# Subtracting the low halves of some weight chunks on Pool instead of DVE

## The chip, the core and the metric

The kernel runs on one core of one Trainium2 chip. The metric is the device time of one execution in microseconds (us); lower is better. TensorE is called PE here, VectorE DVE, ScalarE ACT, GpSimd Pool and SyncE SP, as in the profile.

## What is computed

256 tokens of width 1024 pass through two transformer blocks, all in float32. The first block has adaptive modulation (shift, scale, gate from a vector `c`), a mixer with three kinds of heads, and a convolved, gated feed-forward layer. The second block has grouped-query attention, a squared-ReLU MLP, bidirectional gated linear attention (GLA) and another such MLP. Cut to what matters:

```python
mod = (silu(c) @ w_ada + b_ada)                 # 6 x 1024: shift1, scale1, gate1, shift2, scale2, gate2
h = rmsnorm(x, g_mix) * (1 + scale1) + shift1
proj = h @ w_in                                 # 1024 x 2816, then three kinds of heads
x = x + (1 + gate1) * (concat(y_a, y_b, y_c) @ w_out)
...                                             # w_up 1024 x 5632, conv, silu * value, w_down
qkv = rmsnorm(h, norm_mix[0]) @ attn_w_qkv      # 1024 x 1536, attention, @ attn_w_o
...                                             # MLP: square(relu(h @ mlp_w_in)) @ mlp_w_out, 1024 x 4096
proj = rmsnorm(h, norm_mix[1]) @ gla_w_in       # 1024 x 3104, gated linear attention, @ gla_w_o
...                                             # second MLP, last rmsnorm
```

## The kernel before

**Split weights.** Every large product is made from two parts of each operand: `w_hi` is the weight rounded to PE's float32r format, `w_lo` the rest, `raw - w_hi`. The same is done with the activations. A product is three matmuls, `hi*hi + hi*lo + lo*hi` (helper `three`, lines 1444 to 1446). So a weight chunk cannot be used before its low half is there.

**Chunks.** Weights come as chunks of 1 MB, 128 partitions x 2048 float32. `STREAM` lists them in the order of their loads: 24 chunks of `w_ada`, which only DVE reads (`ada_step`, lines 942 and 945), and 139 chunks for PE (`SPLITS`): 11 of the input projection (`("in", n)`), 4 of the output projection (`out`), 33 of the first feed-forward layer (`gate`, `val`, `down`), 6 of `qkv`, 4 of `wo`, 13 of the GLA input (`gla`; the first is half as wide), 4 of `gla_out`, 64 of the two MLPs. In the input stage a chunk of `in` and one of `ada` alternate.

**The path of a chunk.** SP's queue loads it into one of 4 `raw` slots (line 455). Before it issues the load, it waits until the chunk that lay in that slot is done with: for a PE chunk until its `w_lo` is made, for an `ada` chunk until DVE has added it. SP works strictly in order, so one late slot holds all later loads. ACT copies `raw` to `w_hi` (line 483) into one of 3 split slots, which PE must have left (`chunk_used`). DVE subtracts, `w_lo = raw - w_hi` (line 823). PE then makes 48 matmuls of 128x128 by 256 with it.

**Order on the engines.** `schedule()` is one list of steps, written out by hand; every engine walks it and issues its own part of each step. At a chunk's step, ACT first makes `w_hi` of the chunk two further on (`ahead`, then `weights_upto`), and only then does its share of that step, such as the copies out of PSUM. DVE makes `w_lo` of the chunk one further on (`ahead`, then `weights_lo_upto`). So on DVE a low half stands in the queue behind all the work of the steps before it, though its `w_hi` may have been ready for long; and all that comes after it waits for it. Inside the input stage the work of the heads is woven in (`extra`): rotations (`rope`, lines 1003 to 1014), window attention (`win_a`, 1076 to 1084; `win_b`, 1112), stick-breaking (`stick_a`, 1057 and 1060). In the GLA stage it is the chain `gate(h)` that passes between ACT and DVE (lines 751 to 764 and 1318 to 1336).

**Pool.** Pool makes two memsets at the start (lines 467 and 468) and nothing else.

Of the kernel before, what the change touches and what calls it, by code (L numbers as in the profile page):

```python
# [7 lines left out]
ALU = mybir.AluOpType  # L8
ACT = mybir.ActivationFunctionType
AX = mybir.AxisListType  # L10
F32 = mybir.dt.float32
# [14 lines left out]
RAW_SLOTS = 4  # L26
SPLIT_SLOTS = 3
# [105 lines left out]
LOAD_OF = {key: n for n, key in enumerate(STREAM)}  # L133
SPLITS = [key for key in STREAM if key[0] != "ada"]
# [3 lines left out]
def schedule():  # L138
# [44 lines left out]
    for layer in range(2):  # L183
# [20 lines left out]
        for n in range(MLP_STEPS + 1):  # L204
# [14 lines left out]
LAST_USE = {0: ("in", 10), 1: ("out", 3), 2: ("val", FF_STEPS - 1), 3: ("qkv", 5), 4: ("wo", 3),  # L219
            5: ("mlp_in", 0, MLP_STEPS - 1), 6: ("gla", 12), 7: ("gla_out", 3), 8: ("mlp_in", 1, MLP_STEPS - 1)}  # L220
FIRST_USE = {("in", 0), ("out", 0), ("gate", 0), ("qkv", 0), ("wo", 0), ("mlp_in", 0, 0), ("gla_out", 0), ("mlp_in", 1, 0)}
USES = {"in": 0, "out": 1, "gate": 2, "val": 2, "qkv": 3, "wo": 4, "gla": 6, "gla_out": 7}


def build(nc, a, out, known):
# [3 lines left out]
    with ctx:  # L229
        def sb(name, shape, dt=F32):  # L230
            return ctx.enter_context(nc.sbuf_tensor(name, shape, dt))

        def sem(name):
            if name not in sems:
                sems[name] = ctx.enter_context(nc.semaphore(name))
            return sems[name]

        def mark(name, *event, by=1):

            counts[name] = counts.get(name, 0) + by  # L240
            assert (name, *event) not in marks, (name, event)
            marks[(name, *event)] = (name, counts[name])
            return sem(name), by

        def same(event, as_event):

            assert event not in marks, event
            marks[event] = marks[as_event]

        def at(*event):  # L250

            name, value = (event[0], 1) if known is None else known[0][event]
            return sem(name), value

        raw = sb("raw", [P, RAW_SLOTS, CHUNK])
        w_hi = sb("w_hi", [P, SPLIT_SLOTS, CHUNK], F32R)
        w_lo = sb("w_lo", [P, SPLIT_SLOTS, CHUNK], F32R)
# [100 lines left out]
        def wview(buf, slot, kt):  # L358
            return buf[:, slot, :].rearrange("p (k c) -> p k c", k=kt)

        def halved(buf, slot, key):

            return wview(buf, slot, KT)[:, :, 0:P] if key == ("gla", 0) else buf[:, slot, :]

        def landed(n):
            return at(f"raw_landed{n % RAW_SLOTS}", n)
# [98 lines left out]
        @block.gpsimd  # L465
        def _(pool):
            pool.memset(bqz, 0.0).then_inc(*mark("zeroed", 0))
            pool.memset(cqz, 0.0).then_inc(*mark("zeroed", 1))


        @block.scalar
# [340 lines left out]
        def _(dve):  # L812
            done = {"lo": 0}

            def weights_lo_upto(n):

                while done["lo"] <= min(n, len(SPLITS) - 1):
                    m = done["lo"]
                    key = SPLITS[m]
                    r = LOAD_OF[key]  # L820
                    dve.wait_ge(*landed(r))
                    dve.wait_ge(*at("w_hi", m))
                    dve.tensor_tensor(halved(w_lo, m % SPLIT_SLOTS, key), halved(raw, r % RAW_SLOTS, key),  # L823
                                      halved(w_hi, m % SPLIT_SLOTS, key).bitcast(F32), ALU.subtract)\
                        .then_inc(*mark("w_lo", m))
                    done["lo"] += 1

            def ahead(key, n=1):
                weights_lo_upto(SPLIT_OF[key] + n)
# [147 lines left out]
            def scaled(i):  # L977
                if i == 0:
                    weights_lo_upto(0)
                dve.wait_ge(*at("rstd", i))  # L980
                dve.wait_ge(*at("gains", 2 * i))
                for k in range(KT + 1):
                    if k < KT:
                        dve.scalar_tensor_tensor(out=y_t[:, k, :], in0=x_t[:, k, :], scalar=gain[:, i, k:k + 1],
                                                 in1=rstd[:, :], op0=ALU.mult, op1=ALU.mult)\
                            .then_inc(*mark("normed", i, k))
                    if k > 0:
                        m = 24 * i + k - 1
                        dve.wait_ge(*at("high", SET_OF_NORM[i], k - 1))
                        dve.scalar_tensor_tensor(out=h_lo[:, k - 1, :], in0=y_t[:, k - 1, :], scalar=mod[:, m:m + 1],  # L990
                                                 in1=h_hi[:, k - 1, :].bitcast(F32), op0=ALU.add, op1=ALU.subtract)\
                            .then_inc(*mark("low", SET_OF_NORM[i], k - 1))
# [432 lines left out]
        def _(pe):  # L1425
# [43 lines left out]
            def project_chunk(idx, key, tile=feature_tile, n=2):  # L1469
                if key in FIRST_USE and tile is feature_tile and n == 2:  # L1470

                    slot = weights(key)
                    dst = [take(pe, *key, m)[:, 0:S] for m in range(n)]
                    for k in range(KT):
                        operand(idx, k)
                        for m in range(n):
                            w = [wview(b, slot, KT)[:, k, m * P:m * P + P] for b in (w_hi, w_lo)]
                            ins = three(dst[m], w, (h_hi[:, k, :], h_lo[:, k, :]), k == 0, k == KT - 1)
                            if k == KT - 1:
                                ins.then_inc(*mark("job", *key, m))  # L1480
                else:
                    for m in range(n):
                        tile(idx, key, m)
                used(key, ("job", *key, n - 1))
# [122 lines left out]
            def project(kind, n):  # L1607
                project_chunk(USES[kind], (kind, n))

# [203 lines left out]
```

## Time and profile before

| what | value |
|---|---|
| three runs | 1049.38, 1051.57, 1053.0 us; median 1051.57 |
| the profiled execution | 1053.97 us, of which the span of the trace is 1052.1 |
| busy share | PE 90%, DVE 68%, ACT 48%, Pool 0% |
| mean granted clock of PE | 0.955 |

The span is the time from the first to the last instruction in the trace of one execution. Busy shares are means over stages with different limits. "Idle before" is time in which an engine did nothing, with the engine and instruction that ended it.

### The profile page before, as it was taken

The numbers are of one execution on the slowest core, as the hardware profiler recorded it, in microseconds if no ns is written. First come the engines' busy times: TensorE is split into PE (matmuls) and PEld (weight loads), VectorE is DVE, ScalarE is ACT, GpSimd is POOL, SyncE is SP. The second block draws the span as 40 slices with busy tenths as digits, with TensorE's granted clock in tenths as the row PEclk, the third lists the DMA queues.
The fourth block names the chain that finished last, engine by engine and source line by source line (L and its number), as shares of the span: only waits on it lengthen the run. The fifth ranks groups of instructions, "written<-read, shape, count | busy, mean of one in ns | idle before, by whom it ended". The sixth has DMA issues, their size and how long they took to land.

```text
span 1052.1 us, 17801 instructions
## 1 busy us (share of the span) xinstructions
PE 948.4 (90%) x7373; PEld 914.2 (87%) x7373; DVE 719.2 (68%) x1083; ACT 503.9 (48%) x713; POOL 2.9 (0%) x6
## 2 busy tenths in 40 slices
PE   4499798779999999979999999997988899999997
PEld 3498688779999998965789999997988789999997
DVE  4878586786676769886576566565885867565564
ACT  3325853444554557346554343335656554334332
POOL 1000000000000000000000000000000000000000
PEclk9689898889999999889999999998999899999999
DMA  9867446644555554330246645645442346546531
GB/s 344 309 205 258 145 160 211 229 164 158 201 171 193 193 192 134 121 90 1 81 154 209 213 169 176 214 153 160 125 144 92 98 143 211 189 164 206 192 121 41
DMA packets 122284, 177.14 MB, mean 168 GB/s; under 512 B 3088, under 2 KB 103996, under 8 KB 122076
## 3 DMA queue, kind: packets, MB, share of 16 engines
q1 hardware_dynamic: 121260, 173.97, 49.1%
q10 hardware_dynamic: 944, 2.03, 0.7%
q8 instruction: 59, 0.97, 0.4%
q14 instruction: 21, 0.17, 0.1%
HBM read 174.68 MB, written 1.05 MB: 167 GB/s over the span
## 4 chain that ended last, share of the span: by engine, by line
PE 66%; DVE 19%; ACT 5%; DMA 4%; issue 4%; SPq 1%; DVEq 0%; ACTq 0%
PE psum L1444 20%; PE psum L1445 20%; PE psum L1446 20%; DVE w_lo L823 5%; DVE ada L945 3%; DMA raw<-in_w_ada_dram 2%; PE psum L1712 1%; DMA rows<-in_g_sgu_dram 1%; PE psum L1692 1%; DVE work L862 1%; PE psum L1519 1%; ACT h_hi L494 1%; DMA raw<-in_w_out_dram 1%; DMA raw<-in_w_in_dram 1%; ACT w_hi L483 1%
## 5 line engine op out<-in xcount | busy, mean ns | idle before, releaser
L1444 PE MATMUL psum<-h_hi,w_hi 128*128 128x256 f32 x1384 | 402.2, 291 | 48.2 <-DVE w_lo L823 24.0
L1445 PE MATMUL psum<-h_lo,w_hi 128*128 128x256 f32 x1384 | 397.1, 287 | 0.0
L1446 PE MATMUL psum<-h_hi,w_lo 128*128 128x256 f32 x1384 | 396.6, 287 | 0.0
L483 ACT ACTIVATE w_hi<-raw 128x2048 fp32r<-128x2048 f32 (+1 forms) x139 | 264.4, 1903 | 173.7 <-PE psum L1446 106.7
L1444 PEld LDWEIGHTS psum<-h_hi,w_hi 128*128 128x128 f32 x1384 | 271.3, 196 | 54.1 <-issue 27.4
L823 DVE TENSOR_TENSOR w_lo<-raw,w_hi 128x2048 fp32r<-128x2048 f32 (+1 forms) x139 | 313.1, 2277 | 0.6 <-ACT w_hi L483 0.2
L1446 PEld LDWEIGHTS psum<-h_hi,w_lo 128*128 128x128 f32 x1384 | 270.8, 196 | 0.0
L1445 PEld LDWEIGHTS psum<-h_lo,w_hi 128*128 128x128 f32 x1384 | 270.7, 196 | 0.1
L1444 PE MATMUL psum<-a_hi,w_hi 128*128 128x256 f32 x688 | 192.9, 280 | 0.3 <-DVE w_lo L823 0.2
L1445 PE MATMUL psum<-a_lo,w_hi 128*128 128x256 f32 x688 | 192.3, 280 | 0.0
L1446 PE MATMUL psum<-a_hi,w_lo 128*128 128x256 f32 x688 | 192.2, 279 | 0.0
L1444 PEld LDWEIGHTS psum<-a_hi,w_hi 128*128 128x128 f32 x688 | 129.3, 188 | 0.7 <-DVE w_lo L823 0.7
L1446 PEld LDWEIGHTS psum<-a_hi,w_lo 128*128 128x128 f32 x688 | 129.3, 188 | 0.0
L1445 PEld LDWEIGHTS psum<-a_lo,w_hi 128*128 128x128 f32 x688 | 128.9, 187 | 0.0
L1183 DVE SCALAR_TENSOR_TENSOR arena<-psum,rstd 128x256 f32<-128x256 f32 x64 | 26.8, 424 | 131.2 <-PE psum L1446 130.9
L729 ACT ACTIVATE a_hi<-arena 128x256 fp32r<-128x256 f32 x64 | 26.4, 419 | 114.3 <-DVE arena L1183 114.3
L945 DVE SCALAR_TENSOR_TENSOR ada<-raw,c_act,ada 128x1024 f32<-128x1024 f32 x42 | 53.9, 1283 | 7.6 <-DMA raw<-in_w_ada_dram 6.5
L1152 DVE SCALAR_TENSOR_TENSOR arena<-psum,cols,arena 128x255 f32<-128x255 f32 x44 | 21.2, 481 | 47.2 <-ACT arena L629 33.2
L1444 PE MATMUL psum<-w_hi,h_hi 128*128 128x256 f32 x144 | 43.1, 299 | 5.8 <-DVE w_lo L823 4.1
L1445 PE MATMUL psum<-w_lo,h_hi 128*128 128x256 f32 x144 | 42.1, 292 | 0.0
L1446 PE MATMUL psum<-w_hi,h_lo 128*128 128x256 f32 x144 | 41.9, 291 | 0.0
L1444 PEld LDWEIGHTS psum<-w_hi,h_hi 128*128 128x128 f32 x144 | 29.3, 203 | 7.1 <-DVE w_lo L823 4.7
(262 smaller groups left out, 896.1 us busy)
## 6 DMA issues: line engine op xcount, KB each, us to landing
raw<-in_mlp_w_in_dram SPq DMA_DIRECT2D x32, 1024.0 KB, 5.5
raw<-in_mlp_w_out_dram SPq DMA_DIRECT2D x32, 1024.0 KB, 6.7
raw<-in_w_ada_dram SPq DMA_DIRECT2D x24, 1024.0 KB, 6.7
raw<-in_w_up_dram SPq DMA_DIRECT2D x22, 1024.0 KB, 5.2
raw<-in_gla_w_in_dram SPq DMA_DIRECT2D x12, 1024.0 KB, 5.5
raw<-in_w_down_dram SPq DMA_DIRECT2D x11, 1024.0 KB, 5.5
raw<-in_w_in_dram SPq DMA_DIRECT2D x10, 1024.0 KB, 7.6
raw<-in_attn_w_qkv_dram SPq DMA_DIRECT2D x6, 1024.0 KB, 5.2
```

Source lines behind the costliest of these rows:

```text
L483: act.activation(halved(w_hi, m % SPLIT_SLOTS, SPLITS[m]), halved(raw, r % RAW_SLOTS, SPLITS[m]), ACT.Copy).then_inc(*mark("w_hi", m))
L494: act.activation(h_hi[:, k, :], src, func, **kw).then_inc(*mark("high", idx, k))
L729: act.activation(a_hi[:, 2 * (i % 2) + f, :], ff_g[:, f, :], ACT.Square)\
L823: dve.tensor_tensor(halved(w_lo, m % SPLIT_SLOTS, key), halved(raw, r % RAW_SLOTS, key), halved(w_hi, m % SPLIT_SLOTS, key).bitcast(F32), ...
L862: dve.tensor_tensor(work[:, 0:n, :], work[:, 0:n, :], work[:, n:2 * n, :], ALU.add)\
L945: ins = dve.scalar_tensor_tensor(out=ada[:, p % 2, :], in0=src, scalar=c_act[:, k:k + 1], in1=ada[:, p % 2, :], op0=ALU.mult, op1=ALU.add)
L1152: dve.scalar_tensor_tensor(out=buf[:, f, 1:S], in0=c[:, 0:S - 1], scalar=col("conv_w1", t), in1=buf[:, f, 1:S], op0=ALU.mult, op1=ALU.add)\
L1183: dve.scalar_tensor_tensor(out=ff_g[:, f, :], in0=bank("mlp_in", layer, i, f)[:, 0:S], scalar=0.0, in1=rstd[:, :], op0=ALU.max, op1=ALU.mult)\
L1444: pe.matmul(dst, lhs[0], rhs[0], start=start, stop=False, skip_group_check=True)
L1445: pe.matmul(dst, lhs[0], rhs[1], start=False, stop=False, skip_group_check=True)
L1446: return pe.matmul(dst, lhs[1], rhs[0], start=False, stop=stop, skip_group_check=True)
L1519: ins = pe.matmul(dst[:, k:k + 1], ada[:, p % 2, k * P:(k + 1) * P], cst("ones")[:, 0:1], start=True, stop=True)
```

## The change

The low halves of the chunks of four kinds, `in`, `out`, `qkv` and `gla` (34 chunks of 139), are subtracted on Pool; DVE skips them. The other 105 stay on DVE. Pool walks the 34 chunks in the order of the stream, and waits for each one's load and its `w_hi`. PE's and SP's waits for the low half of these chunks now look at Pool's semaphore. All sizes, slots, steps and the number of instructions stay as they are.

```diff
+POOL_LOW = ("in", "out", "qkv", "gla")
...
 @block.gpsimd
 def _(pool):
     pool.memset(bqz, 0.0).then_inc(*mark("zeroed", 0))
     pool.memset(cqz, 0.0).then_inc(*mark("zeroed", 1))
+    for n, key in enumerate(SPLITS):
+        if key[0] in POOL_LOW:
+            r = LOAD_OF[key]
+            pool.wait_ge(*landed(r))
+            pool.wait_ge(*at("w_hi", n))
+            pool.tensor_tensor(halved(w_lo, n % SPLIT_SLOTS, key), halved(raw, r % RAW_SLOTS, key),
+                               halved(w_hi, n % SPLIT_SLOTS, key).bitcast(F32), ALU.subtract)\
+                .then_inc(*mark("w_lo_by_pool", n))
+            same(("w_lo", n), ("w_lo_by_pool", n))
...
 def weights_lo_upto(n):
     while done["lo"] <= min(n, len(SPLITS) - 1):
         m = done["lo"]
         key = SPLITS[m]
+        done["lo"] += 1
+        if key[0] in POOL_LOW:
+            continue
         r = LOAD_OF[key]
         dve.wait_ge(*landed(r))
         dve.wait_ge(*at("w_hi", m))
         dve.tensor_tensor(...).then_inc(*mark("w_lo", m))
-        done["lo"] += 1
```

## Rows read from the trace of the kernel before

**Rows 1.** The page's first part: busy time, share of the span, instructions.

```profile
PE 948.4 (90%) x7373; PEld 914.2 (87%) x7373; DVE 719.2 (68%) x1083; ACT 503.9 (48%) x713; POOL 2.9 (0%) x6
```

**Rows 2.** Stages: length, then busy time of PE, weight load, DVE, ACT, Pool.

```profile
54.00:105.00 51.00, 48.32 (x350) 46.97 (x351) 41.98 (x64) 20.84 (x35) 0.00 (x0) 0.90 0.73 237
105.00:150.00 45.00, 36.85 (x258) 34.38 (x257) 28.54 (x55) 33.33 (x56) 0.00 (x0) 0.89 0.54 177
150.00:200.00 50.00, 44.10 (x318) 40.71 (x316) 37.11 (x51) 18.36 (x32) 0.00 (x0) 0.90 0.61 211
404.00:462.00 58.00, 47.90 (x355) 46.19 (x355) 51.35 (x93) 26.86 (x50) 0.00 (x0) 0.92 0.39 123
715.00:840.00 125.00, 107.36 (x785) 102.76 (x784) 92.19 (x159) 71.39 (x107) 0.00 (x0) 0.93 0.38 121
```

**Rows 3.** Waits in 50:200, 404:462 and 715:840: total us, times, longest.

```profile
PE psum L1444 <- DVE w_lo L823: 8.1, 4, 3.8
...
PE psum L1444 <- DVE w_lo L823: 2.9, 2, 2.0
...
PE psum L1444 <- DVE w_lo L823: 8.1, 2, 4.1
```

**Rows 4.** PE's timeline: start, length, instruction, idle before it.

```profile
54.14 0.58 PE L1444 MATMUL psum<-h_hi,w_hi 128*128 128x256 f32 x1 [3.78 <-DVE w_lo L823]
...
90.24 0.36 PE L1444 MATMUL psum<-h_hi,w_hi 128*128 128x256 f32 x1 [2.38 <-ACT arena L573]
```

**Rows 5.** Line 1444 in windows of one chunk each (third half a chunk); PEclk follows PEld.

```profile
54.10:62.65 8.55, 5.96 (x16) 4.38 (x16) 0.64 0.76 246
63.30:69.17 5.87, 4.67 (x16) 3.00 (x16) 1.00 0.57 177
90.20:94.70 4.50, 3.08 (x8) 2.26 (x8) 0.62 1.00 354
178.60:185.90 7.30, 5.27 (x16) 3.82 (x16) 0.77 0.83 276
188.60:196.10 7.50, 5.28 (x16) 3.75 (x16) 0.77 0.81 288
422.90:431.40 8.50, 5.90 (x16) 4.38 (x16) 0.65 0.57 181
...
727.00:735.30 8.30, 5.87 (x16) 4.25 (x16) 0.66 0.79 253
780.20:787.40 7.20, 5.24 (x16) 3.77 (x16) 0.76 0.55 165
```

**Rows 6.** SP's queue, whole span, and ACT in 50:200: waits, total us, times, longest.

```profile
SPq L455 <- DVE w_lo L823: 814.5, 124, 58.9
...
ACT w_hi L483 <- DMA raw<-in_w_in_dram: 28.7, 6, 10.3
```

**Rows 7.** DVE's groups by line and form: busy us, mean ns, idle before.

```profile
L823 DVE TENSOR_TENSOR w_lo<-raw,w_hi 128x2048 fp32r<-128x2048 f32 x138 | 312.0, 2285 | 0.6 <-ACT w_hi L483 0.2 <-issue 0.2
```

**Rows 8.** Pool's timeline at the start of the span.

```profile
0.73 1.38 POOL L467 MEMSET arena<- 128x1536 f32 x1 [0.29 <-POOLq L1806]
2.04 1.38 POOL L468 MEMSET arena<- 128x1536 f32 x1
```

**Rows 9.** DVE's timeline, two places.

```profile
38.81 2.29 DVE L823 TENSOR_TENSOR w_lo<-raw,w_hi 128x2048 fp32r<-128x2048 f32 x1
41.02 0.88 DVE L984 SCALAR_TENSOR_TENSOR y_t<-x_t,gain,rstd 128x256 f32<-128x256 f32 x2
...
152.30 2.28 DVE L823 TENSOR_TENSOR w_lo<-raw,w_hi 128x2048 fp32r<-128x2048 f32 x1
```

**Rows 10.** ACT's timeline, two places in the input stage.

```profile
120.39 0.40 ACT L604 ACTIVATE arena<-arena,small 128x128 f32<-128x128 f32 x1 [2.05 <-DVE small L1084]
...
135.30 0.40 ACT L604 ACTIVATE arena<-arena,small 128x128 f32<-128x128 f32 x1 [4.78 <-DVE small L1084]
```

**Rows 11.** DVE's groups in 54:105: the low halves and the additions of `ada`.

```profile
L823 DVE TENSOR_TENSOR w_lo<-raw,w_hi 128x2048 fp32r<-128x2048 f32 x7 | 15.9, 2287 | 0.5 <-ACT w_hi L483 0.2 <-issue 0.2
L945 DVE SCALAR_TENSOR_TENSOR ada<-raw,c_act,ada 128x1024 f32<-128x1024 f32 x10 | 12.8, 1283 | 0.2
```

## The prediction

> **What bounds the kernel now.** I read the page first: PE is busy for 90% of the span, DVE for 68%, Pool for nothing [rows 1]. So over the whole span PE is the limit, and a change on another engine can only win back PE's idle time and the time it runs at the lower clock. Then I cut the span into stages. The reader should see that the stages which the change touches are not PE's best: DVE is busy for 42 of 51 us in 54:105, 37 of 50 in 150:200, 51 of 58 in the qkv stage and 92 of 125 in the GLA stage [rows 2]. Third came the list of waits, by stage: PE stood for a low half for 8.1 us in 50:200, 2.9 us in the qkv stage and 8.1 us in the GLA stage, 19.1 us in all [rows 3]. Last the timelines, for what stood in the queue. The wait at 54.14 is typical [rows 4]: DVE was in the steps before, and the low half came out of its queue late. After such an idle time PE runs at 1.2 GHz for part of the chunk: a chunk that takes 5.87 us at full clock took 8.55, 7.30, 7.50, 8.50, 8.30 and 7.20 us after these waits [rows 5].
>
> **What is taken away.** 33 subtractions of 2.285 us and a half one of about 1.2 leave DVE, 76.6 us [rows 7]. Most of it is hidden behind PE. Where it is not:
>
> 1. Start. The first low half stands in front of `y_t`, from 38.81 to 41.02, and PE waits for what follows [rows 9]: 2.2 us.
> 2. Input stage, second chunk: the wait of 3.78 and 2.7 of lower clock (8.55 less 5.87) [rows 4, 5]: 6.5 us.
> 3. The half chunk at 90.24: 2.38 idle, and 4.50 in place of 2.94 [rows 4, 5]: 4.0 us. The releaser is an ACT copy that stood behind a `w_hi` waiting for its load; loads wait for slots, which DVE frees [rows 6].
> 4. 105 to 160, where ACT's chain and then DVE's sets the order. ACT waits for `win_a` for 2.05 and 4.78 us, with a low half of 2.3 in DVE's queue ahead each time [rows 10]; one more stands at 152.30 in a stretch where DVE has no gaps [rows 9]. I take 2.05 + 2.3 + 2.2 = 6.5 us.
> 5. Output projection: of the 8.1 us of waits, 3.78 is that of item 2 and about 0.2 is small; 4.1 are left, with lower clock of 1.4 and 1.6 [rows 3, 5]: 7.1 us.
> 6. qkv: 2.9, with lower clock of 2.6 (8.50 less 5.87) [rows 3, 5]: 5.5 us.
> 7. GLA: 8.1, with 2.4 and 1.3 of lower clock [rows 3, 5]: 11.8 us.
>
> The sum is 43.6 us, if Pool's subtractions were in time everywhere and disturbed nobody.
>
> **What is added.** Pool gets 34 subtractions. The trace has none. The nearest rows are its memsets of 1536 columns, one every 1.31 us [rows 8], 0.85 ns a column for one stream, so 1.75 us for 2048. A subtraction moves three streams: if all three overlap it takes 1.75, if none does 5.2. DVE takes 2.285 for the same tile [rows 7]. I take 4.4, between two streams one after another (3.5) and three (5.2); both ends stay in the range. The Trainium skill (GPSIMD Engine Reference, 3.1) gives 4497 ns on GpSimd for such an add of 2048 float32, against 2293 on DVE; that would make the sum 34 times 0.1 us of Pool's time longer, and the trace's 2.285 agrees with its DVE half. The longer instruction alone costs little: most low halves are ready for their subtraction 5 us and more before DVE comes to it, and a PE chunk takes 5.87, so Pool keeps pace. The exception is the third chunk of the input stage, whose `w_hi` comes at about 54: its low half comes at about 58.2, PE wants it at 57: minus 1.2. No DMA is added. Behind Pool's waiting instruction only Pool's later subtractions stand; nobody else uses that queue. SP waits for Pool now where it waited for DVE, at 34 of 139 places [rows 6].
>
> **What the two engines do to each other.** This is the unknown, and it decides. No row shows Pool reading SBUF while DVE works. Below, the cost is nothing. Above, a Pool subtraction and any DVE instruction with two operands in SBUF take turns, whole instructions at a time. I see no row that puts it nearer to the lower end, and since a subtraction on either engine needs two read streams at once, I forecast the upper one. What it would then cost, stage by stage:
>
> - Start. Two Pool subtractions (in0, in1) fit into 34.9 to 43.9, and `y_t` starts at 43.9 and not at 41.02: plus 2.9 in place of minus 2.2. But the second chunk is then ready, so item 2 holds. Net minus 3.6.
> - 54:105. DVE's `ada` additions are 12.8 us, their first halves 1.5 and the two-operand parts of `rope` about 6; seven Pool subtractions are 30.8, together 51 in a stretch of 51 [rows 2, 11], where DVE's whole load had been 42. Every pause in a chain of waits now lengthens it: `ada` frees its slots some 5 us later, and SP, in order, loads behind it. I get the sixth chunk 6 us later and the stage's end 4 us later than before: plus 7.6. Item 3 is gone.
> - 105 to 160. Item 4's minus 6.5 stands against five Pool subtractions of 4.4. If the chain meets each at a random point and one in three not at all, that is 7.5 us: plus 1.
> - Output projection: minus 7.1, about 2 lost by later `ada`: minus 5.
> - qkv: minus 5.5; one instruction of the sum tree may be caught behind a Pool subtraction: plus 3. Net minus 2.5.
> - GLA: minus 11.8. In each of four `gate` chains DVE meets a subtraction, for about 1 to 2.5 us: plus 7.3. Net minus 4.5.
>
> Sum: -3.6 + 7.6 + 1 - 5 - 2.5 - 4.5 = -7.0. From the span of 1052.1 that is 1045.1, from the profiled execution's own 1053.97 it is 1047, and from the median of the runs, 1051.57, 1044.6. I forecast 1045.
>
> The Trainium skill has a rule against this change (SBUF — State Buffer, "Who interferes with whom"): a DVE instruction with two SBUF inputs contends with a GpSimd instruction that reads SBUF, and the second to issue is blocked until the first is done. No run here shows it yet. By that rule the sum is -7.0, without it -42.4.
>
> **The rivals.**
>
> *Side by side.* Pool and DVE don't hinder each other. Then 43.6 less the 1.2 comes off, but part of it turns into other waits: ACT already waits 28.7 us for loads of `in` [rows 6], and PE cannot pull those forward. I take off 8: 35 us, 1016. For it: Pool's queue is empty, all 34 low halves come early. Against: nothing in the trace.
>
> *Turns, and at the wrong moments (slower).* The mechanism is the same as in the forecast, the place is 105 to 160. There ACT's and DVE's chain has no slack, and `w_hi` of the next chunk comes from that chain, so Pool's start may fall again and again just ahead of DVE's critical instruction. If all five subtractions delay it whole, they cost 22 and not 7.5: plus 14.5, so 1059.5. It decides from three full hits on. For it: the schedule is fixed, so hits aren't random. Against: many DVE instructions there read PSUM and have only one operand in SBUF.
>
> *Nothing moves* is no case of its own: 76.6 us leave DVE for certain. That it nets to nothing lies between forecast and slower rival.
>
> **How the numbers follow.** Forecast (turns, partly hidden) 0.45, its own range 1036 to 1056; side by side 0.30, 1010 to 1030; slower rival 0.25, 1053 to 1068. What a measurement can tell from no change is 0.3%, 3 us. Faster by over 0.3% (below 1048.4): all of side by side and 0.6 of the forecast, 0.57. Slower (above 1054.7): 0.9 of the slower rival and 0.1 of the forecast, 0.28. Same: 0.15. The range of 8 in 10 leaves a third of the side-by-side case's lower half and the slower rival's top out: 1014 to 1063.
>
> **What would show it.** Pool's 34 instructions near 4.4 us (end of one to start of the next, where they queue). DVE's line 945 at 1.28 as before says side by side; a mean well above, or line 1003 with members of 4 us, says turns. The waits of PE for a low half in 50:200, qkv and GLA should be almost gone; new waits should be for `h_lo`, for `arena` and, on SP, for `ada`. The second chunk of the input stage should follow the first with no gap. The prediction is wrong if Pool's instruction is far from 4.4 us, if DVE is not slowed at all, or if its delays fall into 105 to 160.

## The result, and the profile after

The changed kernel takes 1074.36 us (median of 4 runs, 1072.7 to 1078.89); the kernel before, run beside it, takes 1052.28 (4 runs, 1049.38 to 1053.84). The ratio is 1.022, with a 95% interval of 1.018 to 1.026: slower by 2.2%. I had forecast 1045, a gain, and a range up to 1063: the time went the other way and lies above the range. The profiled execution after took 1075.56 us, with a span of 1073.7.

The first part of the page after, beside [rows 1]:

```profile
PE 952.3 (89%) x7373; PEld 913.5 (85%) x7373; DVE 739.2 (69%) x1049; ACT 503.7 (47%) x713; POOL 161.9 (15%) x40
```

DVE has 34 instructions fewer, which took 76.6 us. Its busy time was to fall from 719.2 to 642.6. It is 739.2, so what stayed on DVE takes 96.6 us longer than before. The same stages as in [rows 2], after (length, then busy time of PE, weight load, DVE, ACT and Pool, then the granted clock):

```profile
54.00:105.00 51.00, 42.53 (x319) 40.07 (x318) 46.46 (x53) 20.47 (x36) 28.38 (x6) 0.90 0.59 199
105.00:150.00 45.00, 35.26 (x237) 32.51 (x236) 27.97 (x36) 28.50 (x46) 14.05 (x3) 0.85 0.47 152
150.00:200.00 50.00, 39.87 (x302) 36.46 (x300) 40.02 (x58) 19.96 (x34) 18.06 (x4) 0.90 0.50 179
404.00:462.00 58.00, 51.31 (x395) 50.03 (x394) 49.78 (x64) 27.88 (x49) 29.29 (x6) 0.94 0.41 139
715.00:840.00 125.00, 111.75 (x847) 106.57 (x846) 84.85 (x131) 66.03 (x93) 59.91 (x13) 0.96 0.42 135
```

The stages lie up to 22 us later now, so the last two windows hold more of PE's dense work from the stage before, and the third is shifted by 12 to 18 us too. The first two compare: PE does less in each of them than before.

PE's waits after, in 50:200, in 404:462 and in 715:840 (total us, times, longest). The waits for a low half of [rows 3] have shrunk from 8.1 to 3.5 in the first stretch and are gone in the second; new ones stand in their place. In 715:840 Pool's low halves still cost 5.2 us, where DVE's had cost 8.1:

```profile
PE psum L1575 <- DVE work L1072: 6.4, 2, 5.5
PE psum L1575 <- DVE arena L1072: 4.9, 3, 2.8
PE psum L1600 <- ACT arena L608: 3.9, 1, 3.9
PE psum L1456 <- POOL w_lo L475: 3.5, 2, 2.1
...
PE psum L1456 <- DVE h_lo L866: 3.3, 1, 3.3
PE psum L1666 <- DVE work L874: 3.3, 1, 3.3
...
PE psum L1456 <- POOL w_lo L475: 5.2, 3, 3.7
```

Which instructions got longer? DVE's groups and Pool's by line and form, after (busy us, mean ns):

```profile
L957 DVE SCALAR_TENSOR_TENSOR ada<-raw,c_act,ada 128x1024 f32<-128x1024 f32 x42 | 78.4, 1867 | 3.5 <-DMA raw<-in_w_ada_dram 2.3
L1228 DVE TENSOR_TENSOR arena<-arena 64x256 f32<-64x256 f32 x16 | 19.3, 1208 | 0.5
L1335 DVE TENSOR_TENSOR work<-work 128x512 f32<-128x512 f32 x4 | 11.4, 2840 | 3.7 <-ACT work L768 3.7
L1096 DVE TENSOR_SCALAR small<-small 128x2 f32<-128x2 f32 x6 | 7.4, 1241 | 0.2
L1195 DVE SCALAR_TENSOR_TENSOR arena<-psum,rstd 128x256 f32<-128x256 f32 x64 | 26.8, 423 | 131.3 <-PE psum L1458 131.0
...
L475 POOL TENSOR_TENSOR w_lo<-raw,w_hi 128x2048 fp32r<-128x2048 f32 (+1 forms) x34 | 159.0, 4689 | 668.4 <-ACT w_hi L493 668.4
```

Before, the additions of `ada` had a mean of 1283 ns [rows 11], the rotations of L1228 one of 420, L1335 one of 692, and L1096, which handles two columns, one of 169. All of them have their operands in SBUF. Set side by side with the trace before, 26 DVE instructions stand for over 1 us, up to 4.4, and make up 92.6 of the 96.6 us. Instructions that read PSUM, such as L1195, and ACT's keep their times.

How one such meeting looks: Pool's timeline after, from 105 to 182, and DVE's in the same stretch.

```profile
109.34 4.62 POOL L475 TENSOR_TENSOR w_lo<-raw,w_hi 128x2048 fp32r<-128x2048 f32 x1 [5.32 <-ACT w_hi L493]
120.00 4.73 POOL L475 TENSOR_TENSOR w_lo<-raw,w_hi 128x2048 fp32r<-128x2048 f32 x1 [6.04 <-ACT w_hi L493]
136.89 4.70 POOL L475 TENSOR_TENSOR w_lo<-raw,w_hi 128x2048 fp32r<-128x2048 f32 x1 [12.16 <-ACT w_hi L493]
153.01 4.54 POOL L475 TENSOR_TENSOR w_lo<-raw,w_hi 128x2048 fp32r<-128x2048 f32 x1 [11.41 <-ACT w_hi L493]
159.00 4.63 POOL L475 TENSOR_TENSOR w_lo<-raw,w_hi 128x2048 fp32r<-128x2048 f32 x1 [1.45 <-ACT w_hi L493]
```

```profile
119.02 6.79 DVE L957 SCALAR_TENSOR_TENSOR ada<-raw,c_act,ada 128x1024 f32<-128x1024 f32 x2
...
135.92 6.76 DVE L957 SCALAR_TENSOR_TENSOR ada<-raw,c_act,ada 128x1024 f32<-128x1024 f32 x2
...
153.54 4.04 DVE L1112 TENSOR_TENSOR small<-small 128x12 f32<-128x12 f32 x1 [3.30 <-ACT small L619]
...
158.23 7.11 DVE L1124 TENSOR_SCALAR arena<-arena,small 128x128 f32<-128x128 f32 x12
```

A pair of `ada` additions takes 2.60 us where nobody disturbs it. The two pairs here take 6.79 and 6.76: in each, the second addition stands until Pool's subtraction, issued during the first, is done. L1112 multiplies 12 columns in 0.17 us before; here it takes 4.04, from 153.54 to 157.58, and Pool ends at 157.55. The twelve instructions of L1124 took 2.84 and take 7.11. So four of the five subtractions in this stretch hit, nearly at full length: 4.2 + 4.2 + 3.9 + 4.3 = 16.6 us.

The starts of PE's chunks say where the 21.6 us of span were lost:

| chunk | before | after | later by |
|---|---|---|---|
| first of `in` | 42.70 | 45.41 | 2.7 |
| second of `in`, its end | 62.8 | 59.07 | -3.7 |
| eighth of `in` | 104.66 | 108.40 | 3.7 |
| first of `out` | 162.39 | 180.16 | 17.8 |
| first of the feed-forward layer | 204.11 | 216.23 | 12.1 |
| first of `qkv` | 405.66 | 420.42 | 14.8 |
| first of `wo` | 510.91 | 531.29 | 20.4 |
| first of `gla` | 719.78 | 740.41 | 20.6 |
| first of `gla_out` | 833.26 | 855.72 | 22.5 |

### The profile page after: what moved, and what is told of

It reads as the page before. It is cut to its first block, busy times and chain, and to the rows that moved or that the text cites. A ratio compares the mean times of both kernels' runs of the same rounds, so it can differ in the third digit from the quotient of the medians.

```text
span 1073.7 us, 17803 instructions
## 1 busy us (share of the span) xinstructions
PE 952.3 (89%) x7373; PEld 913.5 (85%) x7373; DVE 739.2 (69%) x1049; ACT 503.7 (47%) x713; POOL 161.9 (15%) x40
## 4 chain that ended last, share of the span: by engine, by line
PE 65%; DVE 20%; ACT 6%; DMA 4%; issue 3%; POOL 1%; SPq 0%; DVEq 0%; ACTq 0%; POOLq 0%
PE psum L1456 20%; PE psum L1458 19%; PE psum L1457 19%; DVE ada L957 4%; DVE arena L1228 2%; DVE work L874 2%; ACT w_hi L493 2%; PE psum L1724 1%; DVE w_lo L836 1%; POOL w_lo L475 1%; DMA raw<-in_w_out_dram 1%; DMA rows<-in_g_sgu_dram 1%; PE psum L1704 1%; PE psum L1531 1%; DVE h_lo L866 1%
## 5 line engine op out<-in xcount | busy, mean ns | idle before, releaser
L1456 PE MATMUL psum<-h_hi,w_hi 128*128 128x256 f32 x1384 | 397.2, 287 | 41.9 <-DVE h_lo L1002 11.3
L1457 PE MATMUL psum<-h_lo,w_hi 128*128 128x256 f32 x1384 | 393.0, 284 | 0.0
L1456 PEld LDWEIGHTS psum<-h_hi,w_hi 128*128 128x128 f32 x1384 | 266.9, 193 | 47.9 <-issue 25.3
L1457 PEld LDWEIGHTS psum<-h_lo,w_hi 128*128 128x128 f32 x1384 | 266.7, 193 | 0.2
L1458 PEld LDWEIGHTS psum<-h_hi,w_lo 128*128 128x128 f32 x1384 | 266.4, 192 | 0.0
L475 POOL TENSOR_TENSOR w_lo<-raw,w_hi 128x2048 fp32r<-128x2048 f32 (+1 forms) x34 | 159.0, 4689 | 668.4 <-ACT w_hi L493 668.4
L836 DVE TENSOR_TENSOR w_lo<-raw,w_hi 128x2048 fp32r<-128x2048 f32 x105 | 236.7, 2283 | 0.0
L1195 DVE SCALAR_TENSOR_TENSOR arena<-psum,rstd 128x256 f32<-128x256 f32 x64 | 26.8, 423 | 131.3 <-PE psum L1458 131.0
L957 DVE SCALAR_TENSOR_TENSOR ada<-raw,c_act,ada 128x1024 f32<-128x1024 f32 x42 | 78.4, 1867 | 3.5 <-DMA raw<-in_w_ada_dram 2.3
```

The source lines that it names most:

```text
L475: pool.tensor_tensor(halved(w_lo, n % SPLIT_SLOTS, key), halved(raw, r % RAW_SLOTS, key), halved(w_hi, n % SPLIT_SLOTS, key).bitcast(F32), ...
L957: ins = dve.scalar_tensor_tensor(out=ada[:, p % 2, :], in0=src, scalar=c_act[:, k:k + 1], in1=ada[:, p % 2, :], op0=ALU.mult, op1=ALU.add)
L1195: dve.scalar_tensor_tensor(out=ff_g[:, f, :], in0=bank("mlp_in", layer, i, f)[:, 0:S], scalar=0.0, in1=rstd[:, :], op0=ALU.max, op1=ALU.mult)\
L1456: pe.matmul(dst, lhs[0], rhs[0], start=start, stop=False, skip_group_check=True)
L1457: pe.matmul(dst, lhs[0], rhs[1], start=False, stop=False, skip_group_check=True)
L1458: return pe.matmul(dst, lhs[1], rhs[0], start=False, stop=stop, skip_group_check=True)
```

## The experiments

My theory after the result: turns of whole instructions, as forecast, and their price is set by where on the chain each meeting falls. Rivals: Pool's 4.6 us are simply too long for the chunks; the engines share a write path or a queue and not the reads; the cost is spread evenly over the 34.

**Pool writes only.** The low halves are filled with zeros on Pool, for as long as the subtraction takes.

```diff
-pool.tensor_tensor(w_lo, raw, w_hi, ALU.subtract)
+pool.memset(w_lo, 0.0); pool.memset(w_lo, 0.0); pool.memset(first half of w_lo, 0.0)   # one after another
```

> Pool does not subtract here. For each of its 34 chunks it fills the low half with zeros, two and a half times over, so it is busy for about as long as before (2048 + 2048 + 1024 columns at 0.85 ns, 4.4 us and two short waits) but reads nothing from SBUF. The zeros leave the high-low product of these chunks out of the result; all instructions, waits and slots of the other engines stay. Theory (turns: a Pool instruction that reads SBUF and a DVE instruction with two SBUF operands exclude each other): DVE's additions of ada go back from a mean of 1.87 to 1.28 us, nothing on DVE is stretched, and the time falls to the side-by-side case, 1005 to 1030 us. Rival A (the loss is that Pool's low half comes later than DVE's would, 4.6 against 2.3 us): the time stays at 1065 to 1080, since Pool's part takes as long. Rival B (Pool's work loads SBUF whatever it does): DVE stays stretched, and the time near 1074.

This kernel leaves the product with the low halves of these chunks out.

Measured: 1017.67 us (1015.83 to 1020.82), ratio 0.9679 (0.9656 to 0.9702). DVE's and Pool's groups:

```profile
L962 DVE SCALAR_TENSOR_TENSOR ada<-raw,c_act,ada 128x1024 f32<-128x1024 f32 x42 | 53.8, 1282 | 2.6 <-DMA raw<-in_w_ada_dram 1.4
L1233 DVE TENSOR_TENSOR arena<-arena 64x256 f32<-64x256 f32 x16 | 6.7, 420 | 0.5
L1101 DVE TENSOR_SCALAR small<-small 128x2 f32<-128x2 f32 x6 | 5.3, 882 | 0.2
...
L479 POOL MEMSET w_lo<- 128x2048 f32 x33 | 60.3, 1827 | 1.9
L476 POOL MEMSET w_lo<- 128x2048 f32 x33 | 60.2, 1824 | 343.7 <-ACT w_hi L498 343.7
L482 POOL MEMSET w_lo<- 128x1024 f32 x34 | 32.6, 957 | 2.0
```

Pool is busy for 4.6 us per chunk, with the same waits in front, and the kernel gains 3.2%. So neither Pool's length nor its place in the chain costs the time: its reading of SBUF does. `ada` and the rotations are back at 1282 and 420 ns. L1101 is not: 882 against 169, though Pool reads nothing here. That is a second kind of meeting, with an instruction that has a single tensor operand; more of it at the end.

**One kind of chunk at a time.** In each, only the kinds named stay on Pool:

```diff
-POOL_LOW = ("in", "out", "qkv", "gla")
+POOL_LOW = ("in", "out")        # second kernel: ("qkv",), third: ("gla",)
```

> Only the chunks of in and out on Pool. Theory (each stage loses by itself, as the starts of PE's chunks in the two traces say: the first feed-forward chunk starts 12.1 us later in the changed kernel, and nothing there depends on qkv or GLA): before plus 12, so 1064. Rival (the loss of 22 us comes from something that Pool does as a whole, such as the granted clock or its code): plus 22 or nothing.

> Only the six qkv chunks on Pool. Theory: the delay grows by 8.3 us between the end of the feed-forward layer and the first wo chunk, so before plus 8, 1060. It splits into the sum tree that is caught behind a Pool subtraction (3.3 us of idle PE before the sum) and the rotations of q and k (line 1228, mean 1.21 in place of 0.42). Rival (those are hidden, and the shift in the trace of the changed kernel was given on from the input stage): 1047, since PE's waits of 2.9 us with 2.6 of lower clock are gone.

> Only the 13 GLA chunks on Pool. Theory: the delay grows by 1.9 us over the stage, of which minus 6.1 up to the third chunk (the wait of 3.94 and its lower clock are gone) and plus 8 after it, where the gate chain meets Pool: before plus 2, 1054, not to be told from no change. Rival (the gate chain is hidden): before minus 6, 1046.

Measured: 1064.69 (ratio 1.0126, 1.011 to 1.0143), 1057.73 (1.006, 1.0045 to 1.0075) and 1049.89 (0.9991, 0.9979 to 1.0004), beside 1051.29 for the kernel before. `in` and `out` cost 13.4 us, `qkv` 6.4, `gla` nothing that can be measured. There the first of the two waits of [rows 3] is gone (the chunks behind it start 6 us earlier), but the second has only changed its owner, and what DVE loses in the gate chains eats up the rest. PE's waits with `gla` alone on Pool, in 715:840:

```profile
PE psum L1456 <- POOL w_lo L475: 5.1, 3, 3.7
```

The three make 18.4 of the 22.1 lost. The remaining 3.7 is no more than noise allows: the interval of the change's own ratio is 8 us wide.

**The middle of the input stage.** Only the third last to last chunk of `in` and the first two of `out` on Pool, and in a second kernel the other ten of `in` and `out`.

```diff
+POOL_LOW = {("in", 8), ("in", 9), ("in", 10), ("out", 0), ("out", 1)}
 # the other kernel: {("in", n) for n in range(8)} | {("out", 2), ("out", 3)}
```

> Only in 8, in 9, in 10, out 0 and out 1 on Pool, the five whose subtractions fall into 105 to 160. Theory (the term of the forecast that was too small is this one; from the first chunk of that stretch to the first output chunk the delay grows from 3.7 to 17.8 us in the changed kernel): 10 to 15 slower, 1062 to 1066. Rival (the stretch is late only because the input stage ahead of it is late and out of step): plus 1 as forecast, 1052.

> Only the low halves of in 0 to in 7 and of out 2 and out 3 are made on Pool, the other 24 of the change's chunks are back on DVE: what the run with in and out had, less the five middle chunks. If the prices of the places add up, this is what is left of that run: 13 us (in and out, 1064.7 against 1051.3) less 9 to 11 (the middle five, 1058.8 to 1062.8 against 1050 to 1052) is plus 2 to 4, so 1052 to 1056. If the price is one per instruction wherever it stands (two thirds of the 15), it is plus 9, 1060. Side by side outside the middle: 1040. The rows that decide: the start of the chunk in 8, and the mean of line 957.

Measured: the five cost 1058.78 us (1.0104, 1.0073 to 1.0135; 1049.83 for the kernel before), the ten 1055.77 (1.0052, 1.0028 to 1.0075; 1050.1 before). By the medians five chunks cost 9.0 us and the other ten 5.7, three times as much per chunk, and together 14.6 where all fifteen cost 13.4: within the noise the prices of the places add up. The starts of PE's chunks say the same of the place: with the five alone, PE reaches the first `out` chunk at 176.12, 13.7 later than before; with the ten alone at 165.84, 3.5 later; with all fifteen at 179.50, 17.1 later. (The profiled execution of the five was the slowest of its four, 1064.8, so its 13.7 is rather too much.) The five came out 3 us below the range that I expected, the ten at its upper end.

**The subtraction in eight pieces.**

```diff
-pool.tensor_tensor(w_lo, raw, w_hi, ALU.subtract)
+for j in range(0, 2048, 256):
+    pool.tensor_tensor(w_lo[:, j:j+256], raw[:, j:j+256], w_hi[:, j:j+256], ALU.subtract)
```

> All 34 chunks on Pool, each subtracted in 8 pieces of 256 columns. Theory (the two engines take turns by whole instructions, so what hurts is that a DVE instruction of 0.4 us stands behind one of 4.6): a DVE instruction now stands behind 0.6 us at most, DVE's mean for the ada additions falls from 1.87 to about 1.5, and the time falls to between 1030 and 1055, if the 8 pieces together don't take above 6 us. Rival (they share the read path by elements or lines, so that the size of an instruction is of no account): the same 1074 as with whole chunks, or more.

Measured: 1054.24 us (1050.9 to 1057.65), ratio 1.0047 (1.0026 to 1.0068). Pool's and DVE's groups:

```profile
L484 POOL TENSOR_TENSOR w_lo<-raw,w_hi 128x256 fp32r<-128x256 f32 x264 | 218.3, 864 | 324.6 <-ACT w_hi L501 324.6
...
L965 DVE SCALAR_TENSOR_TENSOR ada<-raw,c_act,ada 128x1024 f32<-128x1024 f32 x42 | 59.6, 1419 | 10.1 <-DMA raw<-in_w_ada_dram 8.9
```

A chunk now costs Pool 6.9 us (8 times 0.864) where it cost 4.62, and yet four fifths of the loss are gone. The mean of `ada` falls from 1867 to 1419. Some 100 DVE instructions now stand behind Pool, but 98 of them for 0.6 us or less. That is the opposite of what a Pool that is too slow would give, and what turns of whole instructions give, with two exceptions. At two places an instruction of DVE stands through six or seven of Pool's pieces, which follow each other without a gap:

```profile
725.38 23.09 POOL L484 TENSOR_TENSOR w_lo<-raw,w_hi 128x256 fp32r<-128x256 f32 x32 [3.51 <-ACT w_hi L501]
...
743.78 5.24 DVE L1343 TENSOR_TENSOR work<-work 128x512 f32<-128x512 f32 x1 [1.90 <-ACT work L776]
...
409.08 0.55 PE L1464 MATMUL psum<-h_hi,w_hi 128*128 128x256 f32 x1 [5.34 <-DVE h_lo L874]
```

L1343 takes 5.24 in place of 0.69. The other one is an `h_lo` ahead of the first `qkv` chunk, 3.9 us longer than before; PE stands 5.34 us for it where it stood 1.45. That alone is about what is left of the kernel's loss, 4.4 us. Why DVE gets in between two pieces elsewhere and not at these two places, no run here shows.

**One read stream on Pool.** Pool copies `raw` to `w_lo` two and a half times and reads nothing of `w_hi`; the low half then holds the weight itself and not the rest.

```diff
-pool.tensor_tensor(w_lo, raw, w_hi, ALU.subtract)
+pool.tensor_copy(w_lo, raw); pool.tensor_copy(w_lo, raw); pool.tensor_copy(first half of w_lo, first half of raw)
```

> As the changed kernel, but Pool copies raw to the low half two and a half times (the first gla chunk once) instead of subtracting: the low half then holds the rounded weight and not the rest. Pool reads SBUF with one stream where the subtraction reads with two. Theory (any Pool instruction that reads SBUF excludes DVE's two-operand ones): line 957's mean (it keeps its number but for the added lines) stays well above 1.28, 1.6 or more, and the time is 1060 or more. Rival (only two read streams on Pool do it, as the two streams of DVE do on its side): the mean is 1.28 to 1.3, and the time that of the write-only kernel, 1015 to 1022. Pool's total per chunk should be 4.6 to 6 us either way, so that the two differ by the exclusion alone.

Measured: 1059.59 us (1057.03 to 1061.91), ratio 1.0088 (1.006 to 1.0115). Pool's groups and the `ada` additions:

```profile
L479 POOL CAST w_lo<-raw 128x2048 fp32r<-128x2048 f32 x33 | 70.3, 2131 | 2.1
L476 POOL CAST w_lo<-raw 128x2048 fp32r<-128x2048 f32 x33 | 64.9, 1966 | 359.4 <-ACT w_hi L498 359.4
L482 POOL CAST w_lo<-raw 128x1024 fp32r<-128x1024 f32 x34 | 42.7, 1256 | 2.2
...
L962 DVE SCALAR_TENSOR_TENSOR ada<-raw,c_act,ada 128x1024 f32<-128x1024 f32 x42 | 68.1, 1622 | 5.1 <-DMA raw<-in_w_ada_dram 3.9
```

The mean of 1622 settles it: one read stream on Pool is enough. Against the writing kernel this one differs by the reads (and 0.7 us of Pool's time per chunk), and by 42 us. That it costs less than the subtraction fits the length of a turn, at most about 2 us here and 4.6 there.

**Only where PE waited.** The four chunks whose low half PE had stood for longest in the output and GLA stages go to Pool, nothing else.

```diff
+POOL_LOW = {("out", 2), ("out", 3), ("gla", 1), ("gla", 8)}
```

> Only four chunks on Pool: out 2, out 3, gla 1 and gla 8, the ones for which PE stood longest and in whose time DVE has little to do with two operands in SBUF. Theory: 3.19 and 1.4 of lower clock (out 2), 0.98 and 1.6 (out 3, if its load is not later), 3.94 and 2.4 (gla 1), 4.13 and 1.3 (gla 8) come off, less about 3 for what meets DVE: 12 to 16 us, so 1035 to 1040. Rival (any subtraction on Pool costs DVE as much as it saves): 1049 to 1055.

Measured: 1045.49 us (1040.33 to 1047.18), ratio 0.9957 (0.9939 to 0.9975): faster, but by less than half of what I expected. DVE's timeline shows why:

```profile
162.72 6.78 DVE L957 SCALAR_TENSOR_TENSOR ada<-raw,c_act,ada 128x1024 f32<-128x1024 f32 x2
169.43 2.28 DVE L836 TENSOR_TENSOR w_lo<-raw,w_hi 128x2048 fp32r<-128x2048 f32 x1
```

Pool's subtraction for the third `out` chunk runs from 163.80 to 168.42 and holds the `ada` pair; the low half of the second one, still on DVE, stands behind it, and PE stands 5.21 us for that. The ninth `gla` chunk goes the same way: Pool's subtraction for it, at 761.93, holds an instruction with one tensor operand that takes 0.28 us otherwise:

```profile
761.90 4.73 DVE L1370 TENSOR_SCALAR arena<-arena,small 128x128 f32<-128x128 f32 x1
```

PE no longer waits at the ninth chunk, and stands 6.29 us at the tenth, whose low half is still on DVE.

**The same low halves earlier, on DVE.** No Pool. DVE's queue order is changed at three places: the third `out` chunk's low half right after the sums of the first, that of the second `gla` chunk ahead of the last sums of the first MLP, that of the ninth ahead of the third `keys` step.

```diff
-("project", "out", 0), ("ada", 4, 3), ...
+("project", "out", 0), ("lo", "out", 2), ("ada", 4, 3), ...
-("gla_in", 6), ("keys", 2), ...
+("gla_in", 6), ("lo", "gla", 8), ("keys", 2), ...
-s += [("add_down", "mlp_out", layer)]
+s += ([("lo", "gla", 1)] if layer == 0 else []) + [("add_down", "mlp_out", layer)]
```

> Nothing on Pool; DVE makes three low halves earlier in its order: out 2 right after the first output chunk's sums, gla 1 in front of the last MLP sums, gla 8 in front of keys 2. Theory (the gain that Pool offered was one of place in the queue, not of a second engine): 4.6 (out 2), about 4.5 (gla 1) and 2.5 (gla 8) come off, some 11 us, 1038 to 1044. Rival (DVE is full in these stages, so that what comes earlier pushes as much back): 1048 to 1054.

Measured: 1038.93 us (1037.81 to 1040.49), ratio 0.9903 (0.9883 to 0.9924). PE's waits for a low half in 715:840 fall from 8.1 [rows 3] to 2.4.

**Three more of that kind.**

```diff
-("scaled", 0), ("angles",)
+("scaled", 0), ("lo", "in", 1), ("angles",)
-("root", 1), ("scaled", 1), ("ada", 5, 3)
+("root", 1), ("scaled", 1), ("lo", "val", 0), ("ada", 5, 3)
-[("squares", 3, n) for n in range(4)] + [("tree", 3)]
+[("squares", 3, n) for n in range(4)] + [("lo", "qkv", 2), ("tree", 3)]
```

> As the kernel that makes out 2, gla 1 and gla 8 earlier on DVE, with three more moved forward, nothing on Pool: in 1 before the angles of the rotations (PE stood 3.92 us for it; its w_hi was there), qkv 2 before the sum tree of the second norm (2.03), and val 0 before the last ada step (2.81, of which its w_hi leaves about 1). If waits for a low half cost what they show, with the lower clock behind them, this gives 4 + 2 + 1 and 2 to 4 of clock: 1029 to 1034 against 1038.9. If the work that now stands behind them is as late as they were (angles, then rope and the slots; the tree), nothing: 1037 to 1041.

Measured: 1033.31 us (1031.86 to 1033.94), ratio 0.9835 (0.9811 to 0.986) against 1050.1. It is the fastest kernel here that leaves nothing out, 17 us below the kernel before. But not by my account of it: the second `in` chunk does start at 50.36 in place of 54.14, and the eighth at 104.35 against 104.66, so those 4 us are lost again inside the input stage. The other two gave it: between the kernel with three moves and this one, the first `qkv` chunk goes from 401.19 to 398.47, the third from 418.45 to 413.56, the first `gla` chunk from 716.00 to 708.98.

**One account over all runs.** Before, DVE was busy for 719.2 us. Take off 2.285 for each subtraction moved (1.2 for the half one): that would be its busy time with nobody in its way. What it is busy beyond that, it spent standing inside its instructions:

| on Pool | ratio | DVE busy | DVE stands |
|---|---|---|---|
| all 34 | 1.022 | 739.2 | 96.6 |
| `in`, `out` (15) | 1.0126 | 735.9 | 51.0 |
| `qkv` (6) | 1.006 | 724.6 | 19.1 |
| `gla` (13) | 0.9991 | 716.4 | 25.8 |
| the four of the kernel "only where PE waited" | 0.9957 | 723.0 | 12.9 |
| the middle five | 1.0104 | 729.1 | 21.3 |
| the other ten | 1.0052 | 730.3 | 34.0 |
| 34 in eight pieces | 1.0047 | 697.2 | 54.6 |
| 34, one read | 1.0088 | 723.1 | 80.5 |
| 34, write only | 0.9679 | 656.2 | 13.6 |

A Pool subtraction costs DVE 2.8 us on average (96.6 over 34), more than the 2.285 that it takes off it. And the sum doesn't tell the time: 21.3 us in the middle five cost 9 us, 34.0 in the other ten 5.7, and 25.8 in the GLA stage nothing net.

## Why the prediction was wrong, step by step

- *What is taken away* (43.6, net some 35 if nobody is disturbed): right as a sum. The write-only kernel is nearly that case (DVE stands for 13.6 us in it), and it gives 1017.67 where the rival "side by side" said 1016. With Pool reading, one large term did not come, the second wait of GLA (below).
- *Pool's price*, 4.4 us: measured 4.54 to 4.73 in the five rows above, near it, but by luck: the streams that I added up do overlap, as the last section shows. The figure of the Trainium skill (GPSIMD Engine Reference, 3.1), 4497 ns for an add, came within 5%.
- *Turns, whole instructions*: right, and the choice of the upper end too, but "with two operands in SBUF" was too narrow: two of L1096 and one of L1124, with one tensor operand each, stood for 3.1, 3.4 and 4.3 us. The rule cited from the Trainium skill (SBUF — State Buffer, "Who interferes with whom"), which spoke against the change, agrees with the traces: `ada` 1867 ns with Pool reading, 1282 with Pool only writing.
- *Start*, minus 3.6: the second chunk ends 3.7 earlier. Right. *54:105*, the sixth chunk 6 later and the stage's end 4 later: the sixth starts 6.4 later, the eighth 3.7. Right.
- *105 to 160*, plus 1: this is the step that failed. "If the chain meets each at a random point and one in three not at all, that is 7.5 us" was to be set against item 4's 6.5. The traces show four full hits of five, 16.6 us, and the stretch from the eighth `in` chunk to the first of `out` got 14.1 longer. With 6.5 taken off, 16.6 explains 10 of it. Of the other 4, 1.0 is a load: the stretch begins 3.7 late, and its first `w_hi`, which waits for that load, 4.8 late (107.29, before 102.50). About 3 are PE's clock: after the last of the four hits it had stood for 5.48 us, and ran at about 1.2 GHz then (granted clock 0.54), where it had 1.00 in 150 to 162.4 before. PE after (length, then busy time of PE, weight load, DVE, ACT and Pool, then the granted clock):

```profile
166.30:173.60 7.30, 6.38 (x26) 4.71 (x26) 6.99 (x14) 1.96 (x5) 0.00 (x0) 0.54 0.10 27
```

  The slower rival had the place and nearly the size: five hits of 4.4 less 6.5 is plus 15.5 for this stretch. Its whole time, 1059.5, is still 15 us short, for it left qkv and GLA as forecast. Its own argument, "the schedule is fixed, so hits aren't random", is what decides. In three of the four hits the two engines are started by the same ACT queue within a microsecond: ACT ends L604, which releases DVE's L1069, L1072 and `ada`, and its next instruction is `w_hi`, which releases Pool. ACT's timeline after, at two of them:
```profile
134.34 0.61 ACT L604 ACTIVATE arena<-arena,const 128x384 f32<-128x384 f32 x1
134.86 1.89 ACT L493 ACTIVATE w_hi<-raw 128x2048 fp32r<-128x2048 f32 x1
...
150.95 1.92 ACT L493 ACTIVATE w_hi<-raw 128x2048 fp32r<-128x2048 f32 x1 [3.98 <-DMA raw<-in_w_out_dram]
153.30 0.21 ACT L619 ACTIVATE small<-small 128x12 f32<-128x12 f32 x1
```

  L604 leads to `ada` at 135.92, and `w_hi` to Pool at 136.89. Later `w_hi` leads to Pool at 153.01, and L619 to L1112 at 153.54, right into it. The fourth, L1124, follows the third down DVE's queue. I took a lock step for chance.
- My counter-argument to it, that "many DVE instructions there read PSUM", was true and beside the point: L1069 reads PSUM and is free, but the chain goes on through L1096, `ada` and L1112, which do not.
- *Output projection*, minus 5: PE's start goes from 17.8 late to 12.1 late, minus 5.7. Right, though 1.5 of it is the first chunk's own clock (5.8 us in place of 7.3), which the forecast had not counted.
- *qkv*, minus 2.5: wrong, it came out at plus 8.3 (12.1 late to 20.4). The gain of the third chunk came in part, minus 2.7. The caught sum tree that I priced at 3 is there: DVE's timeline below, 6.63 in place of 2.41. Missed was an `h_lo` (L866) ahead of the first chunk, 1.9 us longer, and with it PE's wait, and the q and k rotations: two of them stand for a pair of Pool's subtractions, 9.27 in place of 0.87, and again 5.09. From the last `qkv` chunk to the first of `wo` PE falls back from 15.4 late to 20.4: its waits for L1253 and L1228 are 0.5 to 1.5 us longer, and some of its work behind them is slower. Pool's and DVE's timelines:

```profile
422.94 5.65 POOL L475 TENSOR_TENSOR w_lo<-raw,w_hi 128x2048 fp32r<-128x2048 f32 x1 [2.95 <-ACT w_hi L493]
440.13 9.34 POOL L475 TENSOR_TENSOR w_lo<-raw,w_hi 128x2048 fp32r<-128x2048 f32 x2 [11.54 <-ACT w_hi L493]
```

```profile
422.96 6.63 DVE L874 TENSOR_TENSOR work<-work 128x1024 f32<-128x1024 f32 x3
...
440.48 9.27 DVE L1228 TENSOR_TENSOR arena<-arena 64x256 f32<-64x256 f32 x2
...
454.61 5.09 DVE L1228 TENSOR_TENSOR arena<-arena 64x256 f32<-64x256 f32 x2
```

  The first row of each also shows both sides of a turn: DVE's first addition of the three held Pool for 1 us (5.65 in place of 4.6), then Pool held DVE's second one for 4.2.
- *GLA*, minus 4.5: came out at plus 2 (20.4 late to 22.5). Of the 11.8 to be taken away the first wait went with its clock, 6.1 (20.6 late to 14.5 at the third chunk). The second did not: PE had stood 4.13 us for DVE's low half of the ninth chunk, and stands 3.70 for Pool's now, whose `w_hi` waits in ACT's queue behind a gate chain (there ACT waits 4.58 for DVE's L1342, before 2.13). L1335 in the gate chains loses 8.6 us (11.4 for 2.8), about the 7.3 that I had for all of them; not counted were the 8.6 that the 128x256 products of L1362 and L1364 lose (15.3 for 6.7), and the 3.6 of L1384, for which PE stands 3.2 us.

```profile
795.01 0.58 PE L1456 MATMUL psum<-w_hi,h_hi 128*128 128x256 f32 x1 [3.70 <-POOL w_lo L475]
```

In one sentence: the mechanism was right, and so were the gains but for GLA's second wait, but the number of meetings was estimated by length of time and not by who starts whom. Forecast minus 7.0, measured plus 21.6; the 28.6 between them are 13.1 in 105 to 160, 10.8 in qkv and attention and 6.6 in GLA, less 1.9 at the other places.

## What to carry to other kernels

When work goes to an engine that excludes another while it runs, a meeting costs the waiting engine what is left of the other's instruction, whatever its own length: 12 columns took 4.04 us. So count the meetings by walking both queues, and look for a common releaser: two instructions that the same engine sets off a microsecond apart met in all three cases traced here. Long instructions on such an engine are worth cutting up even at a loss (eight pieces: 50% more Pool time, four fifths of the loss gone), but that bounds a meeting only most of the time: at two places DVE stood through six or seven pieces in a row.

Where an engine is late and not full, its queue order comes first: moving six subtractions forward on DVE, of which one gave nothing, gave 17 us, about four times the 4.3 of the best set that I tried on Pool.

## What the runs showed of the hardware

**A Pool instruction that only writes still holds some DVE instructions.** With memsets on Pool, `ada` and the rotations (two tensor operands) were free, but TENSOR_SCALAR with one tensor operand in SBUF was not: L1101 (128x2) had a mean of 882 ns against 169, and those of L1129 (L1124 of the changed kernel), in the form of 256 columns, one of 992 against 348:

```profile
L1129 DVE TENSOR_SCALAR arena<-arena,small 128x256 f32<-128x256 f32 x6 | 6.0, 992 | 0.0
```

The Trainium skill has this (SBUF — State Buffer, "Who interferes with whom"): a `tensor_scalar`, copy or cast can run in a mode that takes both of the ports it shares with GpSimd, and then the two block each other for a whole instruction. The traces agree, and show it down to two columns and against a Pool instruction that only writes. I had read the clause on two inputs and counted single-operand instructions as free.

**Pool's speed.** A memset of 2048 columns took 1.83 us, a copy that met nobody 1.90, a subtraction 4.6. So one read stream costs next to nothing beside the write stream, and the second one more than doubles the time. The estimate from [rows 8] that added streams up (two 3.5, three 5.2) would have put the copy at 3.5: that it landed near for the subtraction was luck.
